# PEER sample tokens one place earlier in the order of gather jobs, on one core

## The reference, cut to what matters

```
s1 = einsum('thd,nd->thn', q[..., :PEER_HALF], k1);  s2 = einsum(..., q[..., PEER_HALF:], k2)
v1, i1 = top_k(s1, 16);  v2, i2 = top_k(s2, 16)
cand = v1[..., :, None] + v2[..., None, :]
sc, pidx = top_k(cand, 16)                       # 16 experts for each head
g = softmax(sc)
act = gelu(einsum('td,tkd->tk', x, u_tab[experts]))
out = einsum('tk,tkd->td', g * act, v_tab[experts])
x = x + g2 * out                                 # then a final rmsnorm
```

## Time and profile before

| | |
|---|---|
| median of three runs | 3676.98 us (3673.0 to 3680.94) |
| the profiled execution: its time, its span | 3675.69 us, 3673.6 us |
| PE busy, share of the span | 3118.9 us, 85% |
| DVE busy | 2883.2 us, 78% |
| POOL busy | 1953.4 us, 53% |
| ACT busy | 1363.3 us, 37% |
| data moved by DMA | 1127.20 MB, mean 307 GB/s |

### The profile page before, as it was taken

One profiled execution on the slowest core, in us unless ns is written; L12 is line 12 of the kernel. 1 busy time (PEld: TensorE's weight loads), 2 busy tenths in 40 slices (PEclk: granted clock), 3 DMA queues, 4 the chain that ended last, 5 costly groups with the idle time before them and its releaser, 6 DMA issues.

```text
span 3673.6 us, 56479 instructions
## 1 busy us (share of the span) xinstructions
PE 3118.9 (85%) x17498; PEld 2478.0 (67%) x17498; DVE 2883.2 (78%) x6162; ACT 1363.3 (37%) x3036; POOL 1953.4 (53%) x1504
## 2 busy tenths in 40 slices
PE   7999999999999989488999999999988999995000
PEld 4777776666666668477778888878877888884000
DVE  3333347998888867989899999989999887667898
ACT  4333311222223221287555555555554565000000
POOL 0000013555456654554676767767766775776676
PEclk9999999999999999799999999999999999997555
DMA  7444444777788898778999999999999999999998
GB/s 258 141 133 128 144 150 146 233 240 240 246 290 303 307 343 301 257 270 281 362 389 389 386 383 396 370 358 392 380 344 376 369 409 407 400 411 343 342 353 305
DMA packets 435381, 1127.20 MB, mean 307 GB/s; under 512 B 41888, under 2 KB 174368, under 8 KB 435232
## 3 DMA queue, kind: packets, MB, share of 16 engines
q0 software_dynamic: 204800, 745.10, 54.9%
q1 hardware_dynamic: 225664, 370.51, 28.4%
q10 hardware_dynamic: 4768, 9.96, 0.7%
HBM read 1098.81 MB, written 26.62 MB: 306 GB/s over the span
## 4 chain that ended last, share of the span: by engine, by line
PE 42%; DVE 18%; issue 13%; DMA 11%; POOL 3%; ACT 1%; DVEq 0%; ACTq 0%; POOLq 0%; SPq 0%
PE vacc L2298 15%; PE vacc L888 11%; DVE rows L1714 6%; DMA rows<-in_peer_u,eidx 6%; PE vacc L859 5%; PE scat L2232 3%; POOL rows L1511 3%; DVE oh1w L1793 2%; PE vacc L2212 2%; DMA rows<-in_peer_v,eidx 1%; DMA vbuf<-in_peer_v 1%; DVE htok L1724 1%; PE scat L2285 1%; DVE eidf L1606 1%; DMA rows<-in_peer_v,dots 1%
## 5 line engine op out<-in xcount | busy, mean ns | idle before, releaser
L1511 POOL DMA_INDIRECT rows<-in_peer_u,eidx x1088 | 1428.5, 1313 | 939.7 <-DVE dots L1714 587.9
L1714 DVE CUSTOM_DVE_ANT_0 rows<-rows,htok 128x1024 f32<-128x1024 f32 x1088 | 1349.7, 1268 | 138.7 <-DMA rows<-in_peer_u,eidx 126.0
L2298 PE MATMUL vacc<-W,vbuf 128*128 (+1 forms) x6144 | 1425.1, 387 | 38.3 <-DMA vbuf<-in_peer_v 26.9
L2298 PEld LDWEIGHTS vacc<-W,vbuf 128*128 128x128 f32 x6144 | 1156.8, 192 | 188.8 <-issue 39.8
L2048 ACT ACTIVATE oh<-iota,e2s 128x128 bf16<-128x128 f32 x1536 | 486.5, 391 | 16.1 <-DVE wpart L1764 10.1
L888 PE MATMUL vacc<-W 128*128 128x384 f32 x1280 | 432.7, 494 | 1.2 <-ACTq L763 1.2
L1495 POOL TENSOR_TENSOR hot<-hot,cid 128x864 f32<-128x864 f32 x68 | 129.7, 1911 | 544.8 <-DVE hot L1700 543.6
L1724 DVE SCALAR_TENSOR_TENSOR htok<-rows,dots,htok 128x1024 f32<-128x1024 f32 x256 | 328.9, 1285 | 74.0 <-DMA rows<-in_peer_v,eidx 67.0
L1511 POOL DMA_INDIRECT rows<-in_peer_v,eidx x256 | 305.0, 1191 | 127.0 <-issue 86.5
L888 PEld LDWEIGHTS vacc<-W 128*128 128x128 f32 x1280 | 241.4, 192 | 167.0 <-issue 7.1
L2055 ACT ACTIVATE W<-scat 128x256 f32 (+1 forms) x320 | 122.6, 383 | 581.3 <-PE scat L2285 543.8
(11 more groups left out here) (332 smaller groups left out, 2985.0 us busy)
## 6 DMA issues: line engine op xcount, KB each, us to landing
vbuf<-in_peer_v SPq DMA_DIRECT2D x384, 512.0 KB
W<-in_w_in SPq DMA_DIRECT2D x80, 512.0 KB
W<-in_wq SPq DMA_DIRECT2D x64, 512.0 KB
vbuf<-in_w_ada SPq DMA_DIRECT2D x9, 2048.0 KB, 24.1
rows<-in_peer_u,eidx POOLq DMA_INDIRECT x1088
W<-in_w_in SPq DMA_DIRECT2D x16, 1024.0 KB, 6.5
W<-in_w_ada SPq DMA_DIRECT2D x3, 2048.0 KB, 19.2
W<-in_w_out SPq DMA_DIRECT2D x12, 512.0 KB
```

Of the source, the lines that this page charges most:

```text
L1511: g.indirect_dma_start(rows[:, s, :], None, table[:, :], bass.IndirectOffsetOnAxis(ap=picked, axis=0)).then_inc(landed[s], 16)
L1714: v.tensor_tensor_reduce(rows[:, s, :], rows[:, s, :], htok[:, home, :], 1.0, 0.0, ALU.mult, ALU.add, dots_of(t)[:, c:c + 1]).then_inc(use ...
L2298: mm = pe.matmul(vacc[:, k, :], vbuf[:, s, k * P:(k + 1) * P], W[:, e1, :].rearrange("p o t -> p (o t)"), start=(clear and s == 0 and k % ...
```

## The change

The order of jobs becomes: dots of tile 0 (0 to 127), dots of SAMPLE (128 to 191), dots of tile 1 (192 to 319), sums of SAMPLE (320 to 383), and the rest as before. The plan's rows become m: jobs 12 to 160 (was 148), n: 160 to 350 (was 148 to 320), z: 350 to 384 (was 320 to 346), r: no jobs (was 346 to 384). `expo(0)`, `expo(NGRP)`, `gelu(0)` and `gelu(SAMPLE)` run on ACT inside head 6, `soft_high(0)`, `soft_high(NGRP)` and the sample weights on DVE ahead of head 7. `picks_low(1)` moves to the front of row r. The sample rows are loaded into place 0 of `htok` as soon as tile 0's dots are done, the sample's sums pile up there too, and the places of the later tiles are swapped.

```diff
-TILES = (0, 1, SAMPLE) + tuple(range(2, NT - 1))
+TILES = (0, SAMPLE) + tuple(range(1, NT - 1))
@@ job_starts
-        if t == SAMPLE:
-            sum0[t] = at
-            at += width(t)
+        if t == 1:
+            sum0[SAMPLE] = at
+            at += width(SAMPLE)
-HALF_B, END_B = 148, 320
+HALF_B, END_B = 160, 350
@@ stages
-            ("n", HALF_B, END_B, 12, 12, SLOTS * H // 2), ("z", e, e + 26, 12, 12, 2 * KC),
-            ("r", e + 26, q, 12, 14, 16), ("s", q, q, 14, 15, 8)]
+            ("n", HALF_B, END_B, 12, 12, SLOTS * H // 2), ("z", END_B, q, 12, 12, 2 * KC),
+            ("r", q, q, 12, 14, 16), ("s", q, q, 14, 15, 8)]
@@ mix_scalar (ACT), ahead of the gelu of glru
+            if before_gelu is not None:
+                before_gelu()
@@ places of the rows
-        acc = {SAMPLE: htok[:, 1, :], NT - 3: htok[:, 0, :], NT - 2: htok[:, 1, :]}
+        acc = {SAMPLE: htok[:, 0, :], NT - 3: htok[:, 1, :], NT - 2: htok[:, 0, :]}
+                    home = (t + 1) % 2
-                    sp.dma_start(htok[:, t % 2, :], S["hn2"][t]).then_inc(h_in[t % 2], 16)
+                    sp.dma_start(htok[:, home, :], S["hn2"][t]).then_inc(h_in[home], 16)
@@ POOL
-                    g.wait_ge(used, DOT0[1])
+                    g.wait_ge(used, DOT0[SAMPLE])
-                    if n == DOT0[1] + VD:
+                    if n == DOT0[SAMPLE] + VD - 2:
                         sample_rows()
@@ DVE
                     for f in range(half * H // 2, (half + 1) * H // 2):
+                        if f == H - 1:
+                            soft_high(0)
+                            soft_high(NGRP)
+                            dl_(tile_weights(SAMPLE))
                         mix_vector(v, zB, f, lambda: mixed_step(next(slots)))
                 residual(1)
                 v.wait_ge(lo_out, 32)
-                soft_high(0)
-                soft_high(NGRP)
                 picks_low(0)
-                dl_(tile_weights(SAMPLE))
...
                 residual(3, lambda: mixed_step(next(slots)))
+                summed_rows(SAMPLE)
+                picks_low(1)
                 for n, at in enumerate(steps(plan[5])):
                     mixed_step(at)
-                    if n == 3:
-                        picks_low(1)
                     if n == 8:
                         picks_high(1, nps)
                 scale(2)
                 for at in steps(plan[6]):
                     mixed_step(at)
-                summed_rows(SAMPLE)
@@ ACT
+                def first_picks():
+                    expo(0)
+                    expo(NGRP)
+                    gelu(0)
+                    gelu(SAMPLE)
-                with act.Fori(0, H - 1) as f:
+                with act.Fori(0, H - 2) as f:
                     mix_scalar(act, zB, f, False)
+                mix_scalar(act, zB, H - 2, False, first_picks)
                 mix_scalar(act, zB, H - 1, True)
-                expo(0)
-                expo(NGRP)
-                gelu(0)
                 gelu(1)
-                gelu(SAMPLE)
```

More of the change, by code:

```diff
@@ L109 @@
 TAIL = DOT0[NT - 2] + P // 2
-HALF_B, END_B = 148, 320
+HALF_B, END_B = 160, 350
 def stages():
-    q, e = DOT0[2], SUM0[SAMPLE]
+    q = DOT0[2]
     rows = [("p", 0, 0, 0, 4, 4), ("y", 0, 12, 4, 5, 12), ("m", 12, HALF_B, 5, H + NSU, SLOTS * H // 2),
-            ("n", HALF_B, END_B, 12, 12, SLOTS * H // 2), ("z", e, e + 26, 12, 12, 2 * KC),
-            ("r", e + 26, q, 12, 14, 16), ("s", q, q, 14, 15, 8)]
+            ("n", HALF_B, END_B, 12, 12, SLOTS * H // 2), ("z", END_B, q, 12, 12, 2 * KC),
+            ("r", q, q, 12, 14, 16), ("s", q, q, 14, 15, 8)]
     cuts = [q, q + 28, q + 56] + [q + P + 64 * i for i in range(10)]
@@ L775, in turned_heads, with mix_scalar @@
                 act.sem_inc(qkT_ready, 1)
-        def mix_scalar(act, z, f, last):
+        def mix_scalar(act, z, f, last, before_gelu=None):
             b, fs = z.base, bass.ds(f, 1)
@@ L1704, in dot @@
                 def dot(n, t, c):
-                    s, home = n % VD, 0 if t == SAMPLE else t % 2
+                    s, home = n % VD, 0 if t == SAMPLE else t if t < 2 else (t + 1) % 2
                     if c == 0 and t < 2:
```

## The result

The changed kernel takes 3652.22 us (median of four runs, 3649.68 to 3656.1); the kernel before, beside it, 3675.53. The ratio is 0.9938, 95% interval [0.9926, 0.995]: 23 us faster. The forecast was 3645, range 3630 to 3665.

The account below looks back on a forecast made before the run. PE was taken to bound the last prompt heads and DVE row r. Row r's 45.5 us won less 14.0 of costs gave 31.5, so 3675.7 became 3644.2, plus 1.3 for the median: 3645 us, range 3630 to 3665.

Parts of the forecast that it names:

- Row r: Removing the 38 sums from row r brings quarter -2 forward by 44.2 to 46.8 us, taken as 45.5.
- The narrow wait that I named: In row r, POOL's reload of unit 14, behind gather 385, lands at about 1483, 6 us before it is read.
- Rival (b): In row r the reload of unit 14 or turn(1) comes 8 us later than reckoned: 3653, chance 0.08.
- Heads 0 to 3: Three more jobs each: 4.6 us in all, plus 1.5 us for PE's lower clock (0.64 to 2.34, the slow case).
- The sample rows: In head 3 DVE stands about 3 us for their load, covered by idle time: cost 0.
- rival (c): The sample rows' load queues behind gathers and costs 5 us: 3650, chance 0.08.
- Heads 4 to 6: Extra dots cost 0, hidden in DVE's idle time; gathers 1.5 us over heads 4 to 7; softmax ahead of head 7 1.8.
- Rival (a): Gathers crowd heads 4 to 7, stretching each by 6.8 us, 27 in place of 3.1: 3669, chance 0.14.
- rival (a)'s half case: Gathers stretch heads 4 to 7 by half the full amount: 3656, chance 0.10.
- the sign that was to show rival (a): Heads 4 to 7 at 93 us or more, with DVE waiting for gathers.
- Head 7: Extra jobs make slots 1 to 9 1.6 us late (0 to 5) and delay the last head's rows by 3.0 us.
- Rivals (d) and (e): (d) every moved job lengthens its stage: 3684, chance 0.05; (e) unseen waits and full DMA leave no change: chance 0.03.

Follow-up runs that it names:

- the last run: Changed kernel with softmax moved into head 7, four jobs back in row r, their gathers held, and POOL's unit 13 products held until scale(2) is done: 3639.01 us.
- eighteen_back: Changed kernel with the eighteen jobs of row n put back into row r: 3659.82 us.
- free_places: Changed kernel with seventeen jobs taken from heads 4 to 7, ten put between picks_low(0) and residual(2), seven ahead of picks_high(1) in row r: 3658.75 us.
- twelve_back: Changed kernel with the twelve jobs of row m put back into row r: 3649.85 us.
- order_only: New order of tiles and earlier softmax, with the job plan of the kernel before: 3675.01 us, ratio 1.0002 to the kernel before.
- late_seven_soft: Changed kernel with seven jobs moved from heads 4 to 7 to the slot just ahead of picks_high(1), and the softmax in head 7's first slot: 3644.66 us.

## Why the prediction was right, and where its sum was off

The forecast of 3645 was 7 us low against the median; its range and its sign held. Its own sum was 31.5 us won, and the two profiled executions differ by 26.0: 5.5 of the 7 us. The rest is that the profiled execution was the fastest of four, 2.5 us below their median where the forecast added 1.3.

- **Row r:** forecast 44.2 to 46.8 us, taken as 45.5, measured 44.0. The chain as first added up, 44.2, was right step by step on cross(1)'s clock (19.0 us later than before): unit 14 began at 1508.03, or 1489.0, forecast 1489.1. DVE waits for PE's turn (9.22 us, forecast some 7). `scale(2)` took 1.75 + 7.03 = 8.8 us where I reckoned 5.0 to 7.6. The chance that it would be as fast as `scale(1)` was a misreading of the earlier trace rows: the slow case depends on what POOL does, and the last run showed that.
- **The narrow wait that I named,** the reload of unit 14, did not come: POOL issued its two loads at 1495.00 and 1495.58, the later had landed at 1502.9, and DVE read them at 1508.03 without a wait. Rival (b) is out. On cross(1)'s clock that is 1476.0 and 1483.9, for the 1475 and 1483 that I had worked out.
- **Heads 0 to 3:** 4.6 + 1.5 = 6.1 us forecast, 7.2 measured (1.7 us ahead at L1180 of head 0, 5.5 behind at head 4's first transposes); over heads 1 to 3 it is 6.4, and 6.1 and 6.5 in `eighteen_back` and `free_places`, with the same jobs there. The gap before head 3 grew from 0.83 us to 2.96 (forecast 2.0). Behind it the sixteen products took 7.02 us for 5.33 (granted clock 0.76), 1.7 us more, where the slow case was 2.3 and I charged half:

```profile
914.21 0.82 PE L919 MATMUL scat<-ident,W 128*64 128x128 f32 x6 [2.96 <-issue]
914.86 7.02 PE L890 MATMUL vacc<-W 128*128 128x384 f32 x16
```

- **The sample rows:** landing 5.9 us (4.7 before), DVE stood 3.27 us (forecast 3), and ahead of L1180 in head 3 it still idled 1.54 us. Cost 0, and rival (c) is out:

```profile
936.07 1.23 DVE L1717 CUSTOM_DVE_ANT_0 rows<-rows,htok 128x1024 f32<-128x1024 f32 x1 [3.27 <-DMA htok<-scratch_hn]
```

- **Heads 4 to 6:** 1.5 for the gathers (meant for all four heads) and 1.8 for the softmax, 3.3 us forecast, 8.0 measured in this execution and 4.8 in `twelve_back` with the same jobs in these heads. This is the mis-sized term. The softmax was right: 2.18 us of DVE (1279.40 to 1281.58), 2.1 by `order_only`. The step that failed reads "ahead of L1178 three or four more dots, 3.4 or 4.6 us, stand against some 5.8 of idle", hence cost 0. It counts DVE's instructions and not the time that DVE waits for rows. The changed kernel waits 12.6, 4.8 and 4.4 us for gathers in heads 4, 5 and 6, `twelve_back` 6.3, 9.1 and 5.5; before it was 1.5, 4.0 and 2.1. Of the idle time ahead of L1180 (5.8 to 6.9 us before) 0 to 1.2 are left in both, where three or four dots would leave 1.2 to 3.5. Cover and waits are the same idle time, spent twice. Less the softmax, the term came out at 5.9 us here and at 2.7 in `twelve_back`.
- **Rival (a)** set 27 us for the gathers in place of 3.1 (1.5 and head 7's 1.6). By the same count this execution gives 9.7 (8.0 + 6.9, less 2.2 for the softmax and 3.0 for head 7's sums): more than the forecast and less than the 13.5 of rival (a)'s half case. That case's 3656 lies nearer to the median than 3645 does. Head 4, at 93.98 us with 12.6 of waits, meets the sign that was to show rival (a), the other three heads do not. The share near 0.98 that it reckoned with was not there: head 4 lost most at 0.83.
- **Head 7:** 1.6 + 3.0 = 4.6 forecast, 6.9 measured, 4.4 in `twelve_back`; DVE waited 8.3 us for rows where it had waited 3.5. Row z: 0 forecast, 1.3 us given back.
- Together 7.2 + 8.0 + 6.9 - 1.3, less 1.7 us by which this execution was ahead at head 0, are 19.1 us for the forecast's 14.0. With 1.5 us less in row r and 1.0 us won behind the first batch, for which I have no account, 31.5 becomes the 26.0 measured. Some 4 to 5 us of the 19.1 are head 4's in this one execution. Rivals (d) and (e) are out.

The waits in r were bound by work that had its place in the order, and the jobs that went to the heads cost about half of their DVE time in this execution. What I did not see is what comes next when row r is to be filled again: SP's loads of `wq`, which were late for PE wherever six or seven gathers were issued beside them, and not with one or four.

## What to carry to other kernels

Before a gap of an engine is used as cover, take from it the waits for data that the same jobs will lengthen; with four or five gathers more in a head the waits grew by 0.8 to 11.1 us. Where one head of one execution stands out, look at it in the other kernels that have the same program there before explaining it. A place where DVE idles isn't free for a job that brings a transfer: look at which loads are under way there and at what each is due. Where two engines' instructions slow each other, holding back the one off the path (here POOL's two products) costs one wait.

## What the runs showed of the hardware

**DVE's two-input instructions stand still while POOL multiplies.** `scale(2)`'s eight 128x256 instructions took 7.03 us while POOL's two multiplications ran from 1501.36 to 1505.04; without them 3.26. The difference, 3.8 us, is about POOL's 3.68, and it lies in one instruction: the first of the eight took 4.26 us, the other seven 0.47 each. In `late_seven_soft` five sums beside such products took 9.54 us instead of 6.4, and the products 5.03 for 3.68. The Trainium skill, SBUF — State Buffer, Who interferes with whom, says that DVE and GpSimd share a pair of ports, that a DVE instruction with two SBUF inputs and a GpSimd one that reads SBUF exclude each other, and that the second one stands until the first is done. The traces agree that they exclude each other: 3.26 us with POOL held, 7.03 to 7.16 without. On the order the recorded starts do not bear it out: the instruction recorded at 4.26 us began at 1501.07, 0.29 us before POOL's first product.

**A load of 512 KB took 3.5 to 4.9 us or 10.7 to 13.0 us** (medians to landing of `wq`, 1430 to 1465 us; five kernels with one gather of 512 KB issued in the first 10 us of cross(1), six with six or seven; 7.7 us in `order_only` with four, 16.8 in `free_places`). The fifth load is due some 15 us after the start of cross(1), and SP issues it 4 us after it, when its slot is free.

**POOL's issue of one gather takes between 0.93 and 2.71 us,** with medians near 1.2 us for the rows of `u_tab`; no run separates what decides it.
